# HGRN2 recurrence of a two-layer diffusion step: a projection moved ahead of the turned decays, inner outputs ahead of state products, the last two decay levels in column groups

## What is computed

```
f  = lb + (1 - lb) * sigmoid(pre);   k = 1 - f                 # per token, head and channel
o[t] = sum over s <= t of  (q[t] . prod(f[s+1..t]) k[s]) v[s]  # inside a block of tokens, both directions
     + (q[t] . prod(f[..t])) S                                 # from the state carried into the block
S'   = prod(f[block]) S + sum over s of (k[s] * prod(f[s+1..])) v[s]^T
merged = sum over branches of sigmoid(gate_n) * (o_n @ w_branch[n])
```

## Time and profile before

| what | value |
|---|---|
| median of 3 runs (lowest, highest) | 1878.6 us (1877.42, 1880.3) |
| the profiled execution | 1875.93 us |
| its span, first to last instruction | 1874.0 us |
| busy: PE, DVE, ACT, POOL | 91%, 50%, 19%, 19% of the span |
| mean granted clock of PE | 0.955 of full speed |
| twelve batches of the recurrence | 418.71 us, 22% of the span |
| PE busy in them | 367.23 us |

### The profile page before, as it was taken

How to read it: one execution, slowest core, us unless ns; L and a number is a source line. 1 busy time by engine, 2 the same in 40 slices (tenths; PEclk the granted TensorE clock), 3 DMA queues, 4 the chain that set the end, 5 groups by cost and what they waited for, 6 DMA issues and landing times. The chain is left out here.

```text
span 1874.0 us, 24758 instructions
## 1 busy us (share of the span) xinstructions
PE 1696.2 (91%) x9810; PEld 973.5 (52%) x9810; DVE 945.3 (50%) x2096; ACT 358.9 (19%) x827; POOL 353.7 (19%) x456
## 2 busy tenths in 40 slices
PE   4998999899889979998879999998998999899986
PEld 2554655555556645454346455655655555554443
DVE  0546658968855640010255585788776653210114
ACT  2125510110020031110112462110101102211102
POOL 0000108708700000000000001573573000000000
PEclk8999999999989989999989999998998999899998
DMA  9424032041045427999942300411413443399993
GB/s 377 164 97 181 7 143 98 8 194 76 25 186 224 198 117 298 419 428 426 428 191 70 138 2 29 180 46 68 180 46 151 181 196 152 146 408 428 428 428 155
DMA packets 30507, 361.53 MB, mean 193 GB/s; under 512 B 4296, under 2 KB 5672, under 8 KB 7728
## 3 DMA queue, kind: packets, MB, share of 16 engines
q1 hardware_dynamic: 26416, 341.42, 44.7%
q0 software_dynamic: 3104, 12.13, 1.7%
q10 hardware_dynamic: 864, 6.29, 0.8%
HBM read 352.55 MB, written 15.24 MB: 196 GB/s over the span
## 5 line engine op out<-in xcount | busy, mean ns | idle before, releaser
L982 PE MATMUL bank<-sb_arena,sb_slabs 128*128 128x384 f32 (+3 forms) x2016 | 706.1, 508 | 5.1 <-ACT sb_arena L1621 5.1
L982 PEld LDWEIGHTS bank<-sb_arena,sb_slabs 128*128 128x128 f32 (+2 forms) x2016 | 385.4, 195 | 280.0 <-issue 64.8
L560 PE MATMUL bank<-sb_arena 128*64 128x512 f32 x512 | 159.0, 613 | 11.1 <-DMA sb_arena<-in_W 7.3
L1703 DVE SCALAR_TENSOR_TENSOR sb_arena<-sb_slabs,sb_cv,sb_arena 128x512 f32<-128x512 f32 x238 | 159.1, 745 | 0.0
L2059 POOL DMA_INDIRECT ybuf<-sb_arena,sb_idx x12 | 11.8, 987 | 761.6 <-ACT sb_arena L683 761.6
L560 PE MATMUL bank<-sb_slabs,sb_arena 128*64 128x512 f32 x512 | 154.2, 593 | 0.1
L1679 DVE RECIPROCAL sb_arena<-sb_arena 128x384 f32<-128x384 f32 x22 | 56.1, 2550 | 92.1 <-ACT sb_arena L1446 92.1
L531 PEld LDWEIGHTS bank<-sb_arena 128*128 128x128 f32 x768 | 91.0, 199 | 18.0 <-issue 11.4
L531 PE MATMUL bank<-sb_arena 128*128 128x128 f32 x768 | 94.0, 284 | 6.4 <-DVE sb_arena L735 6.4
L560 PEld LDWEIGHTS bank<-sb_arena 128*64 128x64 f32 x512 | 50.3, 141 | 91.2 <-issue 91.2
L589 PE MATMUL bank<-sb_slabs,sb_arena 128*64 128x512 f32 x352 | 86.2, 602 | 1.8 <-issue 1.8
(11 more groups left out here) (238 smaller groups left out, 1941.0 us busy)
## 6 DMA issues: line engine op xcount, KB each, us to landing
sb_slabs<-in_W SPq DMA_DIRECT2D x114, 2048.0 KB, 13.5
sb_arena<-in_W SPq DMA_DIRECT2D x42, 2048.0 KB, 17.5
ybuf<-in_W POOLq DMA_DIRECT2D x6, 1024.0 KB, 13.2
sb_slabs<-in_W SPq DMA_DIRECT2D x6, 1024.0 KB, 7.6
sb_arena<-ybuf ACTq DMA_DIRECT2D x6, 1024.0 KB, 18.9
sb_slabs<-in_W SPq DMA_DIRECT2D x2, 1152.0 KB, 10.1
sb_xT<-in_xT SPq DMA_DIRECT2D x1, 1536.0 KB, 22.5
out_y<-sb_arena SPq DMA_DIRECT2D x2, 768.0 KB, 3.3
```

Source lines behind the costliest of these rows:

```text
L560: mm = nc.tensor.matmul(ps[half, :], lhsT=hg[:, k, half], rhs=w[i][:, k, :], start=(k == 0), stop=(k == KT - 1))
L982: mm = nc.tensor.matmul(out, lhsT=w, rhs=a, start=(i == 0), stop=(i == n - 1))
L1703: ins = V.scalar_tensor_tensor(sums[:, g, 0:n], w[:, k, 0:n], cv[:, 2 * k + g:2 * k + g + 1], sums[:, g, 0:n], ALU.mult, ALU.add)
```

## The change

Four edits in the recurrence, the same in all twelve batches. The last branch projection gets a fixed place behind A7 and so ahead of kt. oi is written ahead of U. A6 and A7 are cut into 16 products of 32 columns, like A0 to A5, that hold only the pairs which the level needs: 32 x 32 at A6, 32 x 64 at A7. ACT copies them straight to their place in `Am` (six small copies), where DVE placed them under a mask; the mask's table and its load shrink, and DVE's first placing of a batch waits for ACT's copy of `Ac` in the batch before.

```
-        FILL_STEPS = {3: (0, 1, 2, 3, 5), 2: (0, 2, 4)}
+        FILL_STEPS = {3: (0, 1, 2, 3, 5, 7), 2: (0, 2, 4, 7)}
+        def mates(n, g):
+            return (g, NEAR) if n <= N_NEAR else (g ^ NEAR, NEAR) if n == N_NEAR + 1 else (0 if g >= HD else HD, HD)
...
-                                if n > N_NEAR:
-                                    mm = nc.tensor.matmul(ps[:, d * P:(d + 1) * P], lhsT=kk, rhs=qq, start=True, stop=True)
-                                for g in range(0, P if n <= N_NEAR else 0, NEAR):
-                                    mm = nc.tensor.matmul(ps[g:g + NEAR, d * NEAR:(d + 1) * NEAR], lhsT=kk[:, g:g + NEAR], rhs=qq[:, g:g + NEAR], start=True, stop=True)
+                                for g in range(0, P, NEAR):
+                                    mate, w = mates(n, g)
+                                    mm = nc.tensor.matmul(ps[g:g + NEAR, d * w:(d + 1) * w], lhsT=kk[:, g:g + NEAR], rhs=qq[:, mate:mate + w], start=True, stop=True)
...
-                        for half, *m in todo:
-                            half(l, *m)
...
+                        for n in (N_NEAR + 1, N_NEAR + 2):
+                            key = ("A", l, hh, tt, n)
+                            sc.wait_ge(*full(key))
+                            ps = held(key)
+                            for g in range(0, P, LEVELS[n - 1]):
+                                mate, w = mates(n, g)
+                                ins = nc.scalar.activation(Am[g:g + w, :, mate:mate + w], ps[g:g + w, 0:4 * w].rearrange("p (d t) -> p d t", d=4), ACT.Copy)
+                            ins.then_inc(*frees(key))
...
                             if n == 0:
+                                if prev:
+                                    ve.wait_ge(*made("near_placed", (l, *prev)))
...
-                                V.copy_predicated(Am[:, :, :], far_mask[:, n - 1 - N_NEAR, :].unsqueeze(1).broadcast_to([P, 4, P]),
-                                                  ps[:, :].rearrange("p (d t) -> p d t", d=4)).then_inc(*frees(key))
...
-                            place(n)
+                            if n <= N_NEAR:
+                                place(n)
```

More of the change, by code:

```diff
@@ L68 @@
 N_NEAR = 5
-MASKS = N_NEAR * NEAR + (len(LEVELS) - N_NEAR) * P
+MASKS = N_NEAR * NEAR
 GROUPS = ((0, 0, CTX), (1, CTX, T))
@@ L313, in program @@
         near_mask = lmask[:, 0:N_NEAR * NEAR].rearrange("p (n t) -> p n t", n=N_NEAR)
-        far_mask = lmask[:, N_NEAR * NEAR:].rearrange("p (n t) -> p n t", t=P)
         at[0] = EXTRA_AT + EXTRA * SLAB - HEADS * HD
@@ L1292, in _ @@
                                 half(l, *m)
+                        assert not todo
+                        if hh == 0 and tt == 0:
+                            pe.wait_ge(*freed_by(("ic", l, TT - 1)))
                         ps, reader = take(("kt", l, hh, tt))
@@ L1301, in _ @@
                         mm.then_inc(*fills(("kt", l, hh, tt)))
-                        for half, *m in todo:
-                            half(l, *m)
-                        if hh == 0 and tt == 0:
-                            pe.wait_ge(*freed_by(("ic", l, TT - 1)))
+                        ps, reader = take(("oi", l, hh, tt))
+                        if reader:
+                            pe.wait_ge(*reader)
+                        pe.wait_ge(*freed_by(("A", l, hh, tt, len(LEVELS))))
+                        for d in range(4):
+                            h = 4 * hh + d
+                            mm = nc.tensor.matmul(ps[HD * (d % 2):HD * (d % 2) + HD, (d // 2) * P:(d // 2 + 1) * P],
+                                                  lhsT=vC[:, tt, h * HD:(h + 1) * HD], rhs=Am[:, d, :], start=True, stop=True)
+                        mm.then_inc(*fills(("oi", l, hh, tt)))
                         ps, reader = take(("U", l, hh, tt))
@@ L1314, in _ @@
                         mm.then_inc(*fills(("U", l, hh, tt)))
[L1315 to L1323, removed]
                     ps, reader = take(("oe", l, hh))
@@ L1896, in place @@
                             if n == 0:
+                                if prev:
+                                    ve.wait_ge(*made("near_placed", (l, *prev)))
                                 V.tensor_tensor(Ac[:, :, :], near, con[:, SEL:SEL + NEAR].unsqueeze(1).broadcast_to([P, 4, NEAR]), ALU.mult).then_inc(*frees(key))
-                            elif n <= N_NEAR:
+                            else:
                                 V.copy_predicated(Ac[:, :, :], near_mask[:, n - 1, :].unsqueeze(1).broadcast_to([P, 4, NEAR]), near).then_inc(*frees(key))
-                            else:
-                                if n == N_NEAR + 1:
-                                    ve.wait_ge(*made("near_placed", (l, hh, tt)))
-                                V.copy_predicated(Am[:, :, :], far_mask[:, n - 1 - N_NEAR, :].unsqueeze(1).broadcast_to([P, 4, P]),
-                                                  ps[:, :].rearrange("p (d t) -> p d t", d=4)).then_inc(*frees(key))
                             ve.wait_ge(*freed_by(key))
@@ L2138, in constants @@
     mask = []
-    for n, b in enumerate(LEVELS):
-        k, q = (p % NEAR, p[:NEAR]) if n < N_NEAR else (p, p)
+    for b in LEVELS[:N_NEAR]:
+        k, q = p % NEAR, p[:NEAR]
         mask.append((k[:, None] // (2 * b) == q[None, :] // (2 * b)) & (k[:, None] // b != q[None, :] // b))
```

## The result

The changed kernel takes 1862.5 us (median of four runs) where the kernel before takes 1879.4: 0.9905 of it, with a 95% interval from 0.9885 to 0.9924.

What follows compares the result with a forecast made beforehand. Each batch's serial tail and DVE's chain of levels, with PE's granted clock third, set the time. Tails save 46.4 us, less 17.1 (clock) and 14.8 (later levels), is 14.5: median 1864, range 1851 to 1877.

Steps and rivals of the forecast that it cites:

- rival 4: Expert stages: the gain is given back to the DMA queue, median 1878.6; chance 0.13 together with rival 2.
- A tail at full clock: From DVE's last product to the next batch's A0: 5.56 us, or 6.78 in a half's third batch.
- twelve tails at full clock: Ends of all batches: eight of 5.56 and four of 6.78, 71.6 us against 118.05, saving 46.4.
- first charge: Ahead of A7: PE idles, its clock falls and the branch slows; nine tails at 1.9 us, 17.1 us.
- second charge: Second and third batches: POOL starts later against A0, delaying DVE's last product; 14.8 us.
- won in the batches: All twelve batches: 46.4 us saved less charges of 17.1 and 14.8, so 14.5 us.
- 2 us and more: PE's idle time ahead of A7 in second and third batches, counted as making their tails slow.
- Rival 2: Levels: DVE and POOL set the batch under full lock; -1 us, median 1879; chance 0.13 together with rival 4.
- The steps on the way: Expected trace signs: batch lengths, idle time moved ahead of A7, A7 about 0.5 us, oi not waiting for ACT.
- Rival 1: Tails: the clock holds except in third batches; 24 us won, median 1854.6; chance 0.23.
- rival 3: Tails: the clock's fall covers branch, kt and U in every batch; -9 us, median 1888; chance 0.08.

Runs made afterwards that it cites:

- a1: The changed kernel run again unaltered, beside the variants on the same chip: 1860.6 us, 0.9892 of the kernel before.
- e7: The changed kernel with two buffers for the decayed keys in turn, so POOL no longer waits for kt: 1851.7 us, 0.9849 of the kernel before.
- e3: The changed kernel with U put ahead of oi again, as before the change: 1859.0 us, 0.9885 of the kernel before.
- e5: The changed kernel with the last branch one step earlier, between A6 and A7: 1860.0 us, 0.9889 of the kernel before.

## Why the prediction was right

**What bounds the kernel** was read rightly: 18.2 us saved in the batches are 18.5 in the span (15.5 and 14.1 in a1), so little or nothing went back to the DMA queue (rival 4), whose slices look as in the earlier trace rows.

```profile
DMA  9424033051045528999941300411414533499993
```

**The terms of the sum.** A tail at full clock was put at 5.56 us and measured 5.75 to 5.78; a third one at 6.78, and 7.03 in e7, where one ran at a clock of 1.00:

```profile
510.92:517.95 7.03, 5.53 (x60) 1.00 0.39 107
```

| term | forecast | measured |
|---|---|---|
| twelve tails at full clock | 71.6 | 8 x 5.76 + 4 x 7.03 = 74.2 |
| first charge, the clock | 9 x 1.9 = 17.1 | 85.9 - 74.2 = 11.7, seven tails |
| second charge, later levels | 14.8 | (118.05 - 85.9) - 18.2 = 14.0: 12.2 in second and third batches, 1.8 in a first one |
| won in the batches | 14.5 | 18.2 (a1: 15.5) |

That the median came within 1.5 us of the forecast is partly luck. The tails were put 2.6 us too low, the clock 5.4 too high and the later levels 2.6 too high in the batches that the forecast named; a first batch, put at nothing there, took 1.8. These errors cancel in part.

The clock's term was too large in both factors. A slow tail costs 1.65 us (7.39 and 7.45 against 5.75), since its branch takes 4.07 to 4.54 and not up to 5.24. And the second batch of layer 0's first half kept its clock behind 2.17 us, and the first ones of second halves behind 1.5. "2 us and more" was no sure sign: 2.17 us gave either result in the same kernel, and in a1 it was another second batch that kept its clock, behind 2.63.

**The second charge** has nearly the right size, 12.2 us for 14.8, but its shares were put wrongly, and its cause holds in a part of the batches. Second batches lost 2.1 to 2.7 us (forecast 2.1), third ones of second halves 1.9 and 2.0, those of first halves nothing (24.2 against 24.7 in the earlier trace rows, forecast 1.6). POOL starts 1.6 us ahead of A0 (forecast 1.7). The forecast let POOL's length behind that start set the product. This fits where POOL ended 0.3 us ahead of the product, in the second batches of first halves (338.03 and 338.31) and the third ones of second halves. In the second ones of second halves POOL ended 1.4 us ahead, and in the third ones of first halves 2.5 us behind the product, so there it was not POOL's end that set it. That DVE's start also hangs on kt, by way of U, is not in the forecast, and e7 speaks for DVE in the second batches. What is shown is the time from kt to the next product; how POOL and DVE share it is open. Rival 2's full lock did not come to pass. In the second batches of first halves two of the last level's four operations met POOL's wide products, at 1.19 and 1.48 us; the other two took 0.42:

```profile
336.83 1.48 DVE L430 TENSOR_TENSOR sb_arena<-sb_arena 64x256 f32<-64x256 f32 x1
```

**The steps on the way.** First batches lost 2.4 to 5.3 us (forecast 3 to 5), second ones of a first half got 0.1 and 1.9 longer (forecast 0 to 2). A7 took 0.65 with its drain; oi did not wait for ACT, and U waited 0.19 for its copy. Rival 1 (24 us) had the clock hold in all but the third batches, and three second batches fell; rival 3 falls, since kt and U behind a slow branch ran at 0.60 and 1.08, as at full clock.

**Where the reasoning fell short.** The sum counted oi under ACT's copy as a gain of the tail and gave it back, unnamed, in the later levels. The two cancel in second and third batches, e3 shows. With the time from kt to the next product in view, the effect is simpler: the branch leaves the place behind kt, where it had given POOL 3.8 to 6.3 us of lead over A0. Without it the last product comes some 2 us later in six of eight batches, which is less than the tails win.

## What to carry to other kernels

Find the loop that sets a stage, and not only the serial rows at its end: here kt releases POOL and, by way of U, DVE, and a constant later the next product is due, so oi behind U is free and work ahead of kt is not. Move one step and another step's worth may change (oi's place: nothing with the branch ahead of kt, 6 us without). A saving that leaves an engine waiting elsewhere is to be followed to where its clock falls next: e5 took 12.7 us out of the batches, 10 came back behind them, and 3.5 of these lie where the clock fell.

## What the runs showed of the hardware

- The same 2.17 us of idle time ahead of the same instructions left the branch at 2.85 us in one layer and 4.54 in the other, and 2.63 us left it at 4.53 in the result and at 2.85 in a1; a fall that was avoided ahead of A7 came at U and oe instead (1.86 for 1.08, 1.98 for 1.09).
- 16 products of 32 or 64 columns in column groups (32 records) take 0.46 or 0.65 us with their drain, but 224 such records in a row were broken by 1.95 us in which PE waited for nothing that the profile shows. A7's 32 records start within 0.58 us (306.23 to 306.81), 18 ns each; the floor of about 25 ns in the Trainium skill (TensorE: Matmul & The Clock Gate, "Wait — 56ns, not 53.3ns?") disagrees with this row too.
- DVE's 256-wide product with two SBUF inputs took 0.41 us alone, 0.83 to 1.05 beside POOL's products of the same size, and 1.37 beside its 512-wide ones.
